# Heads of the second mixer normed among mLSTM tiles; w_ada tiles in the pauses of five norms

## Chip, cores, metric

One core of a Trainium2 chip. The metric is the device time of the whole program in microseconds, the median of several runs; lower is better. Everything is fp32 at the inputs and outputs.

## What is computed

A trunk of two layers over 256 tokens and 256 context tokens of width 1024, and then a second block. Cut to what matters:

```python
# first block, layer l = 0, 1
sh1, sc1, gt1, sh2, sc2, gt2 = split(silu(c) @ w_ada + b_ada, 6)      # for c and c_ctx
x = x + gt1 * (mix(modulate(rmsnorm(x, g1), sh1, sc1)) @ w_out)
x = x + gt2 * conv_ffn(modulate(rmsnorm(x, g2), sh2, sc2), w_up, conv_w, w_down)
...
x = rmsnorm(x, final_g)
# second block: its own w_ada; mLSTM in two directions and window attention, then PEER
h = modulate(rms(x, g), sh1, sc1);  p = h @ w_in
q, k = rope(rms(heads(p.q), q_g)), rope(rms(heads(p.k), k_g))
a = window_attention(q, k, v, kc, vc, sink);  m = mlstm(p)
x = x + g1 * ((sigmoid(g_m) * (m @ w_bm) + sigmoid(g_a) * (a @ w_ba)) @ w_out)
x = x + g2 * peer(modulate(rms(x, g'), sh2, sc2), w_query, keys, u, v)
```

## The kernel before, in words

Activations stand transposed, features on partitions, tokens along the free axis. Every large weight is read as tiles of 128 x 1024 fp32 (512 KB), one tile giving 128 output features over eight groups of 128 inputs. A product is made of three fp32r matmuls per group (`mm3`, L86): high times low, high times high, low times high parts. So each tile is *split* after it has landed: ScalarE rounds it into TH (`highs`), and VectorE or, for tiles flagged so, GpSimd subtracts into TL (`lows`). A tile takes 24 matmuls of 256 columns, or 48 with 512 tokens.

`weight_tiles` (L227) writes the order of all tiles by hand, and every engine's program follows it. SyncE issues all the transfers on one queue into RAW, a ring of four places (`sync_program`, L2518): tile i waits until tile i-4 has been split or, if it isn't split, used. TH and TL have three places each, and a split waits until the tile three splits before has been used by TensorE. `pool` in `add` says which tiles GpSimd subtracts.

The 144 tiles of w_ada (three blocks of 48) aren't split: each gives 8 plain fp32 matmuls with two stationary columns, all into one PSUM bank (`ada`). After each group of four, ScalarE copies the bank to AROW, and at the start of the next group TensorE and VectorE turn it into columns with the bias added (`columns`; a few groups, ADA_TURNED, L358, have that called elsewhere). `_ada_plan` (L333) says at which points of the program how many tiles stand: "head", "unit" (attention units), "between", "up" and "down" (feed-forward), "second", "heads", "lstm".

A norm: ScalarE squares eight rows, GpSimd adds the first five, TensorE sums over partitions with one-column matmuls (`norm`), VectorE adds epsilon (`above`), GpSimd takes the power -0.5 (`root`), TensorE spreads the root over partitions (`spread`), VectorE multiplies row by row (`norm_rows`), ScalarE modulates and rounds (`high_rows`), VectorE subtracts the low part. The next projections start with `project_side`, which takes three tiles' first rows together while the normed rows come.

The second mixer begins behind the final norm. `project_side` takes wg (gates), tile 20 (keys) and 21 (values); then come the query tiles 16 to 19. Each of the five heads' tiles (20, 16, 17, 18, 19; `HEAD_TILES`, L220) is copied by ScalarE, squared, summed (`head_stats`), gets its root on GpSimd, is spread (`head_spread`), normed by VectorE, and roped: a permuting matmul (`head_rope` on TensorE), then three VectorE operations. Before the change all of this stands in front of the attention units, in an order written out by hand in each engine's program (TensorE L922, ScalarE L1464, VectorE L2066, GpSimd L2499). The GpSimd program splits the next head's tile before it takes each root, if the tile is its.

Then come 16 attention units (`a_units`). In unit n TensorE turns the probabilities, does `scores2(n + 2)`, one mLSTM tile (`mlstm_tile(n)`, order `M_TILES`: four q, four output gates, four k, four v), one w_ada tile, and the product with the values. VectorE does `softmax2(n + 2)`, `keep2`, one step of the mLSTM recurrence (steps 0 to 4 in units 0 to 4), the copy of the tile, and `normal2(n + 2)`. Units 0 to 7 have tiles of 24 matmuls, 8 to 15 of 48. All PSUM banks but one are a ring of seven in program order. Each engine works strictly through its own program; semaphores connect them.

Line numbers in the rows are those of helpers: L79 and L84 are the matmuls, L107 transposes, L114 VectorE's or GpSimd's two-operand operation, L120 tensor_scalar, L126 scalar_tensor_tensor, L155 and L158 ScalarE's activation and copy, L2540 the weight transfers.

## Time and profile before

| | us |
|---|---|
| median of 3 runs | 2296.83 (2292.07, 2296.83, 2296.93) |
| the profiled execution's own time | 2286.08 |
| its span, first to last instruction | 2284.3 |
| TensorE busy | 2156.3 |
| VectorE busy | 1292.8 |
| ScalarE busy | 1088.5 |
| GpSimd busy | 488.4 |
| mean granted TensorE clock | 0.973 of full |

The span ends with 128 + 128 tiles of PEER experts, from about 1450 us on, in which TensorE is hardly ever idle. What the change touches lies between 287 and 1446 us. Busy times of TensorE are those of records whose ends are modelled, so consecutive matmuls overlap a little.

### The profile page before, as it was taken

How to read it: one execution, taken by the hardware profiler on the slowest of the kernel's cores; microseconds unless marked ns; L12 is line 12 of the kernel's file. 1: busy time of each engine (PE TensorE's matmuls, PEld its weight loads, DVE VectorE, ACT ScalarE, POOL GpSimd, SP SyncE). 2: the span in 40 equal slices, each digit the busy share in tenths (PEclk: the TensorE clock that was granted, in tenths of full speed). 3: DMA queues.
4: the chain of work that ended last, by engine and by line, in shares of the span. 5: the costliest groups of instructions: out<-in, count | busy, mean ns of one | idle time of the engine just before them, and what ended most of it. 6: DMA issues, size and time to landing. Idle time of an engine off the chain costs nothing.

```text
span 2284.3 us, 44523 instructions
## 1 busy us (share of the span) xinstructions
PE 2156.3 (94%) x19132; PEld 2030.5 (89%) x19132; DVE 1292.8 (57%) x2517; ACT 1088.5 (48%) x1880; POOL 488.4 (21%) x230
## 2 busy tenths in 40 slices
PE   4999999999999989998789998999999999999998
PEld 3977989999998779988668888999999999999998
DVE  2355454343344667555464455589568887666665
ACT  2343353232235446445333444565567776555554
POOL 0200100000002220001201343078866662000000
PEclk8999989999999999999879999999999999999999
DMA  7224323444454345764223334555544445555553
GB/s 279 76 101 155 123 93 130 163 152 166 167 171 151 125 154 181 247 231 137 77 93 130 129 102 150 165 185 188 182 139 148 148 140 174 187 186 189 187 185 130
DMA packets 97284, 355.01 MB, mean 155 GB/s; under 512 B 10688, under 2 KB 11712, under 8 KB 96704
## 3 DMA queue, kind: packets, MB, share of 16 engines
q1 hardware_dynamic: 97088, 352.18, 46.0%
q8 instruction: 150, 2.46, 0.4%
q14 instruction: 46, 0.38, 0.1%
HBM read 351.09 MB, written 1.05 MB: 154 GB/s over the span
## 4 chain that ended last, share of the span: by engine, by line
PE 82%; DVE 5%; issue 4%; ACT 4%; DMA 3%; POOL 2%; SPq 0%; ACTq 0%; DVEq 0%; POOLq 0%
PE ps L79 77%; PE ps L84 4%; ACT TH L158 2%; DVE TL L114 2%; POOL TL L114 1%; PE ps L107 1%; DMA RAW<-in_wdn 1%; DMA RAW<-in_wada 1%; ACT SQ L155 1%; DMA RAW<-in_wup 1%; POOL SM L114 1%; DMA RAW<-in_win 0%; ACT Hh L158 0%; DVE ps L114 0%; DVE X L126 0%
## 5 line engine op out<-in xcount | busy, mean ns | idle before, releaser
L158 ACT ACTIVATE TH<-RAW 128x1024 fp32r<-128x1024 f32 (+1 forms) x515 | 539.9, 1049 | 447.0 <-PE ps L79 190.8
L114 DVE TENSOR_TENSOR TL<-RAW,TH 128x1024 fp32r<-128x1024 f32 (+1 forms) x339 | 416.0, 1227 | 503.0 <-ACT TH L158 502.5
L114 POOL TENSOR_TENSOR TL<-RAW,TH 128x1024 fp32r<-128x1024 f32 x176 | 424.2, 2414 | 545.5 <-ACT TH L158 519.4
L79 PE MATMUL ps<-Hh,TL 128*128 128x256 f32 x1920 | 453.4, 289 | 42.3 <-ACT Hh L158 18.8
L79 PE MATMUL ps<-Hh,TH 128*128 128x256 f32 x1920 | 441.3, 282 | 0.0
L79 PE MATMUL ps<-Hl,TH 128*128 128x256 f32 x1920 | 440.5, 282 | 0.0
L79 PEld LDWEIGHTS ps<-Hh,TL 128*128 128x128 f32 x1920 | 325.0, 193 | 71.4 <-issue 30.5
L79 PE MATMUL ps<-HXh,TL 128*128 128x256 f32 x1312 | 365.6, 283 | 6.8 <-POOL TL L114 2.8
L79 PE MATMUL ps<-W,TH 128*128 128x256 f32 x2048 | 361.9, 281 | 0.0
L79 PE MATMUL ps<-HXh,TH 128*128 128x256 f32 x1312 | 360.0, 278 | 0.0
L79 PE MATMUL ps<-HXl,TH 128*128 128x256 f32 x1312 | 359.8, 278 | 0.0
L79 PEld LDWEIGHTS ps<-Hh,TH 128*128 128x128 f32 x1920 | 325.4, 193 | 0.7 <-issue 0.5
L79 PEld LDWEIGHTS ps<-Hl,TH 128*128 128x128 f32 x1920 | 325.2, 193 | 0.0
L79 PEld LDWEIGHTS ps<-W,TH 128*128 128x128 f32 x2048 | 312.5, 188 | 0.0
L79 PE MATMUL ps<-W,TL 128*128 128x256 f32 x1024 | 287.8, 281 | 1.5 <-DVE G L114 1.5
L79 PEld LDWEIGHTS ps<-HXh,TL 128*128 128x128 f32 x1312 | 246.8, 190 | 9.1 <-POOL TL L114 3.7
L79 PEld LDWEIGHTS ps<-HXh,TH 128*128 128x128 f32 x1312 | 246.0, 189 | 0.0
L79 PEld LDWEIGHTS ps<-HXl,TH 128*128 128x128 f32 x1312 | 245.5, 189 | 0.0
L79 PEld LDWEIGHTS ps<-W,TL 128*128 128x128 f32 x1024 | 196.6, 192 | 1.7 <-DVE G L114 1.7
L114 POOL TENSOR_TENSOR ACC<-SQ 128x512 f32<-128x512 f32 (+1 forms) x6 | 7.7, 1290 | 591.5 <-ACT SQ L155 591.5
L155 ACT ACTIVATE W<-W,T 128x128 fp32r<-128x128 f32 x256 | 82.0, 391 | 64.4 <-DVE W L114 64.4
L84 PE MATMUL ps<-RAW,SM 128*2 128x128 f32 x2304 | 93.7, 287 | 16.2 <-DMA RAW<-in_wada 16.2
(323 smaller groups left out, 3003.1 us busy)
## 6 DMA issues: line engine op xcount, KB each, us to landing
RAW<-in_wada SPq DMA_DIRECT2D x144, 512.0 KB, 3.6
RAW<-in_ut SPq DMA_DIRECT2D x128, 512.0 KB, 3.5
RAW<-in_v SPq DMA_DIRECT2D x128, 512.0 KB, 3.5
RAW<-in_wup SPq DMA_DIRECT2D x88, 512.0 KB, 4.4
RAW<-in_win SPq DMA_DIRECT2D x74, 512.0 KB, 4.4
RAW<-in_wdn SPq DMA_DIRECT2D x32, 512.0 KB, 4.4
RAW<-in_wout SPq DMA_DIRECT2D x24, 512.0 KB, 3.7
RAW<-in_wq SPq DMA_DIRECT2D x16, 512.0 KB, 4.3
```

What stands on the lines that cost most here:

```text
L79: return self.e.matmul(out, lhs, rhs, start=first, stop=last, skip_group_check=skip)
L84: return self.e.matmul(out, lhs, rhs, start=first, stop=last, tile_position=at)
L107: return self.e.transpose(out, src, eye)
L114: return DRY if self.e is None else self.e.tensor_tensor(out, a, b, op)
L155: return DRY if self.e is None else self.e.activation(out, a, fn, **kw)
L158: return DRY if self.e is None else self.e.activation(out, a, ACT.Copy, **kw)
```

## The change

It does two things. (1) Twelve w_ada tiles move into the pauses of five norms: two or one (`z` = 0) stand between a norm's sums and its spread, as many (`z` = 1) between the spread and the first projection. Layer 0's second norm has four, the other four norms (layer 1's first and second, the second block's first and second) two each. They come out of layer 0's up and down projections (4), layer 1's units (2) and down projections (4), the point "second" (1) and the mLSTM part (1). In these pauses ScalarE and VectorE split no tiles ahead for them. `columns(11)` is no longer called apart, and `columns(35)` stands behind the queries of PEER. (2) The heads of the second mixer: mLSTM tiles 0 and 1 come between the heads' tiles 17 and 18, head 3's norm begins before unit 0 and ends in unit 1, tile 19 with head 4 stands in units 0 to 3, and units 1 to 14 carry the other mLSTM tiles, unit 15 none. Of these tiles GpSimd splits 20 and every second one from tile 2 on; 16, 17, 0, 1, 18 and 19 are VectorE's, which also does the gate rows behind the first head's sum.

```diff
@@ weight_tiles
+    def gap(*norm):
+        for z in range(2):
+            ada("gap", *norm, z)
...
             add(("win", l, i), win[i], pool=2)
+            if l and i == 16:
+                gap("n1", l)
...
                 add(("wup", l, m), ins[f"wup{l}"][m])
+                if m == 1:
+                    gap("n2", l)
...
-    ada("second")
-    add(("wg",), ins["wg2"], pool=2)
-    for i in HEAD_TILES[0:1] + (21,) + HEAD_TILES[1:]:
-        add(("w2", i), w2[i], pool=2)
+    add(("wg",), ins["wg2"])
+    add(("w2", 20), w2[20], pool=1)
+    add(("w2", 21), w2[21])
+    gap("n1", 2)
+    for i in FILLS2[0:5]:
+        add(("w2", i), w2[i])
     ada("heads")
     for u in range(16):
-        add(("w2", M_TILES[u]), w2[M_TILES[u]], pool=2)
+        for i in fill2(u):
+            add(("w2", i), w2[i], pool=1 if u % 2 else False)
         ada("unit", 2, u)
...
+            if m == 2:
+                gap("n2", 2)
+FILLS2 = HEAD_TILES[1:3] + M_TILES[0:M_EARLY] + HEAD_TILES[3:5] + M_TILES[M_EARLY:]
+def fill2(u):
+    return FILLS2[5 + u:6 + u]
@@ tensor_program, at each of the five norms
+            ada("gap", "n2", l, 0)
             spread(("n2", l), ROOT[0][:, 0:NTB], 1, D, "h_norm", "m2", l, 7)
+            ada("gap", "n2", l, 1)
@@ tensor_program, second mixer
+        head_tile(1)
+        head_stats(0)
+        turn_rows(1, 4, (2, "vt", 0), A, "vt")
+        head_tile(2)
+        head_spread(0)
+        head_stats(1)
+        mlstm_tile(0)
+        head_rope(0)
+        head_spread(1)
+        head_stats(2)
+        mlstm_tile(1)
+        head_rope(1)
+        head_spread(2)
+        head_tile(3)
+        ada("heads")
+        scores2(0)
+        head_rope(2)
+        head_stats(3)
+        scores2(1)
         for n, (c, kv, qb) in enumerate(a_units):
...
-            mlstm_tile(n)
+            if n == 0:
+                head_tile(4)
+                head_spread(3)
+            elif n + M_EARLY <= 16:
+                mlstm_tile(n + M_EARLY - 1)
+            if n == 1:
+                head_rope(3)
+                head_stats(4)
+            elif n == 2:
+                head_spread(4)
+            elif n == 3:
+                head_rope(4)
@@ vector_program, second mixer
+        lows(at_tile["w2", 16])
+        head_above(0)
+        lows(at_tile["w2", 17])
+        for g in range(4):
+            gate_row(g)
+        lows(at_tile["w2", 0])
+        head_norm(0)
+        head_above(1)
+        head_rope(0)
+        lows(at_tile["w2", 1])
+        head_norm(1)
+        mlstm_tile(0)
+        head_above(2)
+        lows(at_tile["w2", 18])
+        head_rope(1)
+        head_norm(2)
+        mlstm_tile(1)
+        lows(at_tile["w2", 19])
+        ada("heads")
+        softmax2(0)
+        head_rope(2)
+        head_above(3)
+        softmax2(1)
+        normal2(0)
+        normal2(1)
         for n in range(16):
             if n + 2 < 16:
                 softmax2(n + 2)
             if n:
                 keep2(n - 1)
+            if n == 0:
+                head_norm(3)
+            elif n == 1:
+                head_rope(3)
+                head_above(4)
+            elif n == 2:
+                head_norm(4)
+            elif n == 3:
+                head_rope(4)
             if n < 5:
                 for d in range(2):
                     recurrence(d, n)
-            mlstm_tile(n)
+            for i in fill2(n):
+                lows(later(("w2", i), AHEAD))
+            if n and n + M_EARLY <= 16:
+                mlstm_tile(n + M_EARLY - 1)
@@ gpsimd_program
+        lows(at_tile["w2", 19])
         for c in range(5):
-            lows(at_tile["w2", HEAD_TILES[min(1 + c, 4)]])
             root(("head", c), ROOT[2 + c % 2][:, 0:4 if c else 8])
+            if c > 2:
+                lows(at_tile["w2", FILLS2[c + 3]])
```

ScalarE's program follows the same order.

## Rows read from the trace of the kernel before

**Rows 1.** The page's first part: busy us (share of the span), instructions.
```profile
PE 2156.3 (94%) x19132; PEld 2030.5 (89%) x19132; DVE 1292.8 (57%) x2517; ACT 1088.5 (48%) x1880; POOL 488.4 (21%) x230
```
**Rows 2.** TensorE's waits over the span: us in total, times, longest.
```profile
PE ps L79 <- POOL TL L114: 20.3, 8, 6.7
...
PE ps L107 <- DVE mprob L120: 5.7, 2, 4.0
```
**Rows 3.** Timeline at layer 1's first norm: start us, us, engine, instruction [idle before].
```profile
710.17 4.65 POOL L114 TENSOR_TENSOR TL<-RAW,TH 128x1024 fp32r<-128x1024 f32 x2
710.25 2.07 PE L79 MATMUL ps<-P,SM 128*128 128x128 f32 x8 [1.35 <-POOL SM L114]
...
712.54 2.64 SPq L2540 DMA_DIRECT2D RAW<-in_win  x3
...
715.08 0.77 PE L79 MATMUL ps<-Hh,TL 128*128 128x256 f32 x2 [2.75 <-ACT Hh L158]
```
**Rows 4.** Windows of lower clock at five norms: length, busy us per engine, clock, DMA.
```profile
709.53:719.77 10.24, 6.77 (x30) 6.50 (x31) 6.02 (x9) 6.56 (x13) 5.29 (x3) 0.50 0.44 155
...
1074.76:1081.59 6.83, 5.30 (x34) 4.44 (x35) 1.71 (x6) 1.79 (x4) 4.20 (x4) 0.50 0.00 1
...
sum 44.38, PE 31.90 PEld 30.18 DVE 25.89 ACT 27.25 POOL 11.42; mean PE 6.38 PEld 6.04 DVE 5.18 ACT 5.45 POOL 2.28
```
**Rows 5.** Windows: the heads' stretch; its last lower-clock stretch; all four of those.
```profile
1102.80:1193.50 90.70, 66.69 (x462) 51.09 (x460) 47.41 (x115) 28.52 (x56) 18.93 (x10) 0.77 0.23 76
...
1180.58:1190.81 10.23, 7.66 (x31) 5.74 (x32) 8.30 (x28) 4.22 (x12) 0.00 (x0) 0.50 0.16 51
sum 40.95, PE 29.39 PEld 22.37 DVE 17.02 ACT 10.00 POOL 6.13; mean PE 7.35 PEld 5.59 DVE 4.25 ACT 2.50 POOL 1.53
```
**Rows 6.** Timeline: one w_ada tile in dense work, one in a norm's pause.
```profile
680.03 0.62 PE L84 MATMUL ps<-RAW,SM 128*2 128x128 f32 x16
...
1080.16 1.03 PE L84 MATMUL ps<-RAW,SM 128*2 128x128 f32 x16
```
**Rows 7.** Transfers: issues of w_ada, KB each, median us to landing.
```profile
RAW<-in_wada SPq DMA_DIRECT2D x144, 512.0 KB, 3.6
```
**Rows 8.** Window in layer 1's down projections; the last number is GB/s.
```profile
984.00:1016.00 32.00, 28.78 (x324) 25.43 (x322) 11.89 (x17) 8.85 (x11) 0.00 (x0) 1.00 0.66 230
```
**Rows 9.** Timeline in front of head tile 17.
```profile
1098.49 3.22 DVE L126 SCALAR_TENSOR_TENSOR X<-X,SM,ps 128x256 f32<-128x256 f32 x8
...
1105.92 2.67 POOL L114 TENSOR_TENSOR SM<-SM 128x8 f32<-128x8 f32 x1 [22.51 <-DVE SM L120]
...
1110.95 0.58 PE L79 MATMUL ps<-Hh,TL 128*128 128x256 f32 x1 [6.71 <-POOL TL L114]
```
**Rows 10.** Timeline at head 0's rope: spread, rope operation, sums, a split by VectorE.
```profile
1120.95 0.66 PE L79 MATMUL ps<-P,SM 128*64 128x128 f32 x8
...
1121.13 0.42 DVE L114 TENSOR_TENSOR SQ<-ps,C 128x256 f32<-128x256 f32 x1 [3.06 <-PE ps L79]
...
1121.54 0.61 PE L79 MATMUL ps<-P,SQ 128*128 128x2 f32 x4
...
1122.73 1.21 DVE L114 TENSOR_TENSOR TL<-RAW,TH 128x1024 fp32r<-128x1024 f32 x1
```
**Rows 11.** The chain: start us, us, dense matmuls of 256 columns.
```profile
1912.75 362.06 PE ps L79 x3072
```
**Rows 12.** Timeline of the recurrence's second step in unit 2 and 3.
```profile
1168.91 0.41 DVE L120 TENSOR_SCALAR mkeep<-mkeep 4x512 f32<-4x512 f32 x1
...
1170.82 2.61 POOL L114 TENSOR_TENSOR TL<-RAW,TH 128x1024 fp32r<-128x1024 f32 x1 [29.95 <-ACT TH L158]
...
1171.31 2.66 DVE L114 TENSOR_TENSOR mvm<-mvm 4x512 f32<-4x512 f32 x1
...
1180.22 0.68 DVE L114 TENSOR_TENSOR mkm<-mkm 4x512 f32<-4x512 f32 x1
```

More of the change, by code:

```diff
@@ L220 @@
 HEAD_TILES = 20, 16, 17, 18, 19
+M_EARLY = 2
 class Box:
@@ L333, in _ada_plan, with gap @@
 def _ada_plan():
+    def gap(n, *norm):
+        return [(("gap",) + norm + (z,), n) for z in range(2)]
     plan = [(("head", 0), 8), (("head", 1), 8)]
     plan += [(("unit", 0, u), 24 * (u + 1) // 16 - 24 * u // 16) for u in range(16)]
+    plan += gap(2, "n2", 0)
     for third in range(3):
         for m in range(8 * third, min(8 * third + 8, 22)):
-            plan += [(("between", 0, m), 1)] * (m >= 12) + [(("up", 0, m), 1)]
-        plan += [(("down", 0, third, m), 1) for m in range(8)]
-    plan += [(("unit", 1, u), 10 * (u + 1) // 8 - 10 * u // 8) for u in range(8)]
-    plan += [(("down", 1, third, m), 1) for third in range(2) for m in range(8)]
-    plan += [(("second",), 1), (("heads",), 1)]
+            plan += [(("between", 0, m), 1)] * (m >= 12) + [(("up", 0, m), 1)] * (m > 1)
+        plan += [(("down", 0, third, m), 1) for m in range(8 if third < 2 else 6)]
+    plan += gap(1, "n1", 1)
+    plan += [(("unit", 1, u), 1) for u in range(8)]
+    plan += gap(1, "n2", 1)
+    plan += [(("down", 1, 0, m), 1) for m in range(8)] + [(("down", 1, 1, m), 1) for m in range(4)]
+    plan += gap(1, "n1", 2)
+    plan += [(("heads",), 1)]
     plan += [(("unit", 2, u), 1) for u in range(16)]
-    plan += [(("lstm", u), 1) for u in range(4)]
+    plan += [(("lstm", u), 1) for u in range(3)]
+    plan += gap(1, "n2", 2)
     at, n = {}, 0
@@ L1202, in ada, with gap @@
                     act.act(SC, par(["c1", "c2"][b]), ACT.Silu).then_inc(*A.mark("sc", b + 1))
+        def gap(*norm):
+            for z in range(2):
+                ada("gap", *norm, z)
         def stats(tag, src, t, *ready):
@@ L1517, in mlstm_tile @@
                 to_rows((2, "vm", c), ("w2", tile), 512, (c + 1) % 2, *free)
-        for n in range(2):
-            exps2(n)
+        head(0)
+        highs(at_tile["w2", 17])
+        to_rows((2, "vt", 0), ("w2", 21), 512, 1, (D, "h_low", "m1", 2, 7))
+        sq_read[1] = P, "row", 2, "vt", 0
+        highs(at_tile["w2", 0])
+        act.wait_ge(P, "row", 2, "vt", 0)
+        act.copy(m.vt, ps("row", 2, "vt", 0)[:, :].rearrange("p (b c) -> p b c", c=128)).then_inc(*A.mark("vt"))
+        head(1)
+        highs(at_tile["w2", 1])
+        head(2)
+        highs(at_tile["w2", 18])
+        highs(at_tile["w2", 19])
+        ada("heads")
+        head(3)
+        exps2(0)
+        highs(at_tile["w2", 2])
+        exps2(1)
         for n in range(16):
@@ L1695, in ada, with gap @@
                     columns(g)
+        def gap(*norm):
+            for z in range(2):
+                ada("gap", *norm, z)
         def scales(tag, l, name, part, slot):
@@ L2034, in vector_program, with gate_row @@
         dve.memset(m.ONE, 1.0).then_inc(*D.mark("one"))
-        for g in range(4):
+        def gate_row(g):
             d = g // 2
@@ L2170, in mlstm_tile @@
                 rows_v(c - 1)
-        for n in range(2):
-            softmax2(n)
-            normal2(n)
+        lows(at_tile["w2", 16])
[16 more added lines that the diff above has]
+        lows(at_tile["w2", 19])
+        ada("heads")
+        softmax2(0)
[4 more added lines that the diff above has]
+        normal2(1)
         for n in range(16):
```

101 lines of the change are left out of this document (27 added, 74 removed).

## The prediction, made before the change was run

> **What bounds the kernel now.** I read the page's first lines, then TensorE's waits over the span, then the norms' timelines and granted clock, last the stretch with the second mixer's heads. TensorE is busy 2156.3 us, the next engine, VectorE, 1292.8 [rows 1]. So the time is TensorE's own work, what it waits for, and what its work loses while the lower of the clock's two levels (1.2 instead of 2.4 GHz) is granted. Its largest wait is for splits made by GpSimd, 20.3 us in eight waits; the one for normalised probabilities is 5.7 in two, of which one is 4.0 and so the other 1.7 [rows 2]. Two places hold most of what can be won.
>
> The norms: TensorE idles before the root comes and again before the first normed row, 1.35 and 2.75 us at layer 1's first norm [rows 3]. Around the five norms that the change touches the clock is at its lower level for 44.4 us, in which TensorE is busy 31.9 [rows 4]. Dense work loses half of its time there, one-column sums less; I put the loss at 12 us.
>
> The heads: from 1102.8 to 1193.5 TensorE is busy 66.7 of 90.7 us, so it idles 24.0. In four stretches at the lower clock it is busy 29.4, of which half, 14.7, is loss [rows 5]. Together 38.7 us.
>
> The profiled execution took 2286.1 us, 1.8 more than its span and 10.7 below the median of the three runs, 2296.8. The sum is made against 2286.1, and the gain is then taken off the median. About 0.2% (4.6 us) is what a measurement of this kernel can tell from no change.
>
> **Part 1: w_ada tiles in the pauses.** Twelve of the 144 tiles stand in pauses afterwards. One (called second) did already, so eleven leave dense stretches. A tile is 0.62 us long there [rows 6], less the 0.07 by which records of TensorE overlap (a spread from 1120.95 takes 0.66 and the next matmul is there at 1121.54 [rows 10]): 11 x 0.55 = 6.0 us. In a pause it costs nothing as long as the wait beside it is longer. At the lower clock it takes 1.03 [rows 6], and the pauses before and after the spread are 1.35 and 2.75 [rows 3]; layer 0's has two tiles in each half, which the cover just holds. The cover is GpSimd's root and the first rows of VectorE and ScalarE; if it went, the eleven tiles would cost what they cost now.
>
> A tile must also have landed. RAW has four places, so the second tile of a pause takes the place of the norm's first weight tile once that is split. In front of the up projections, of the second mixer and of wq VectorE makes that split before the root is asked for, and a w_ada tile lands 3.6 us after its issue [rows 7]: in time. At layer 1's first norm GpSimd makes it, behind the root: two splits back to back in 4.65 us from 710.17, the first done at 712.5, where SyncE issues the next tile [rows 3]. The pause's second tile then lands at 716.1 and takes 1.0: the projections begin at 717.2 instead of 715.08. **Cost 2.1 us**; bounds 0 (it lands sooner) and 3 (the low clock goes on for as long again over dense work). What is behind it on SyncE's queue is weights not needed for 30 us.
>
> Layer 1's down projections carry 12 tiles instead of 16. They move 230 GB/s and idle 3.2 of 32 us [rows 8]. I give the relief of the transfers 1 us, between 0 and 2.
>
> The clock in the pauses: at the one norm that has a tile in its pause the lower level ended at 1081.59, with the pause's own work; at layer 1's first norm, with none, it went on to 719.77, over 4.7 us of dense work from 715.08 [rows 3, 4, 6]. So a filled pause gives the clock back earlier. The ends are 0 and 12 us. I take 4, because the one-column sums ahead of the root, in which it falls, stay.
>
> **Part 2: the heads among the tiles.** TensorE's work stays; what changes is what each split waits for.
> - Tile 17. VectorE did eight rows of the final norm (3.22 us) and the gate rows before the first head's sum; GpSimd took the root (2.67) and then the split, and TensorE waited 6.71 for it until 1110.95 [rows 9]. Now VectorE makes the split directly behind that sum, and the gate rows follow. The sum's matmuls end about 1103.7, sum and split take 1.4, TensorE arrives at 1104.2: wait 1.1. Queued behind are tile 0's split (in time with TensorE, bank 0.3 late) and the recurrence, not needed yet.
> - Tile 18 before, tile 1 now. VectorE has a rope (3 x 0.42) and the split (1.21) to do behind TensorE's rope matmul, while TensorE has a spread and sums, 0.66+0.61 [rows 10]: wait 1.2. Behind that rope waits tile 1's split and so one RAW place; TensorE then has tile 1 to do, 24 matmuls at 362.06/3072 us, 2.8 [rows 11].
> - Unit 0. A rope (1.3) stands between VectorE's two first softmaxes now: 1.7 becomes 3.0 [rows 2, 10].
> - Unit 4. The recurrence's second step holds VectorE from 1168.91 to 1180.90, and TensorE waited 4.0 for the probabilities behind it [rows 2, 12]. Now VectorE must first norm head 4, whose spread comes behind a tile (2.8+0.66 after the scores; it started 1.6 after them), and do tile 13's split: about 2.4 and 1.2 more, against a spread and a rope more on TensorE, 1.2. **Wait 6.4.** But one addition of the step took 2.66 where its twin took 0.68, beside a split of 2.61 on GpSimd [rows 12]. Tile 12's split comes earlier now, so I expect that back: 4.4. Between them I take 5.5.
> - The recurrence's columns, needed by TensorE right after unit 4's scores: 1.0.
>
> Waits 1.1+0.3+1.2+3.0+5.5+1.0 = 12.1 instead of 24.0: 11.9 saved. Clock: unit 4's fall stays (half of 7.66 busy, 3.8 [rows 5]); of falls at tile 17 and at unit 0 I count one, 3.4: 7.2 instead of 14.7, 7.5 saved. The part brings 19.4. Ends: 9 (waits nearly as before, or the clock) and 27.
>
> On that addition of 2.66: the Trainium skill (SBUF — State Buffer, section "SBUF: two separate sides") says that VectorE, with two SBUF inputs, and GpSimd take their shared port pair as a lock for a whole instruction. The trace agrees: the addition ended 0.5 us after the split did. By the rule the wait is 4.4 and the sum 1 us better; with the delay put down to chance it is 6.4 and 1 us worse.
>
> **Sum.** 6.0 - 2.1 + 1 + 4 + 19.4 = 28.3 us: 2257.8 for an execution like the profiled one, **2269** against the median.
>
> **Rivals.**
> A, *VectorE paces the heads.* Its queue alternates ropes, which wait for TensorE, with splits, for which TensorE waits. With 3 us at each of five heads, 3 at unit 0, 8.5 at unit 4 and 1 behind it, waits are 27.5, and with 11 of clock the heads bring nothing. Part 1 is left, 9 us: 2288. For it: VectorE works 47.4 of the 90.7 us [rows 5] and gets three more splits. Against: its split takes half of GpSimd's. Chance 0.13.
> B, *slower: the clock stays down through the head units.* Place: tile 17 to unit 4. TensorE's work at full speed is 52 us (90.7 - 38.7). If attention's part-array matmuls and short waits keep the lower level throughout, that is 104, plus 12 of waits: 26 more than now, less 9 from part 1: 2314. It decides from some 70 us of lower clock on; now there are 41 [rows 5]. Against: three tiles in a row are dense work. Chance 0.06.
> C, *the clock holds*: only unit 4's fall is left in the heads, and the pauses get most of theirs back: 28 + 3 + 8 = 39, and 2 from shorter waits: 2256. Chance 0.13.
> D, *every pause tile is late* by a landing, 3.6: 18 less at five norms, 2287. Against: where VectorE splits, the place is free in time. Chance 0.06.
>
> **How the numbers follow.** The forecast has 0.62; its own range is 2259 to 2282, for its terms' bounds don't all fall on one side. To leave out no more than 2 in 10 the range takes in C, D and A: 2255 to 2288. Faster by over 0.2% (below 2292.2) are the forecast, C, D and A, less something for a mishap I can't see: 0.87. Same 0.06. Slower, B and a remainder, 0.07.
>
> **What would show it.** Right: the two long waits for GpSimd's splits (6.71 and its neighbour) gone; the heads' stretch, measured to the same tile, 19 us shorter; a wait of 4 to 7 us for normalised probabilities at unit 4; a wait of 1 to 2 us for RAW<-in_wada at layer 1's first norm and at no other; low-clock stretches at the norms shorter than 44.4 in sum. Wrong: waits of 2 us and more for VectorE's splits at tiles 0, 1 and 18; the lower level over most of the units; waits for w_ada at several norms.

## The result, and the profile after

| | before | after |
|---|---|---|
| median, us | 2294.45 (4 runs, 2289.30 to 2296.93) | 2260.76 (4 runs, 2259.18 to 2263.05) |
| profiled execution, us | 2286.08 | 2259.43 |
| its span, us | 2284.3 | 2257.6 |

After / before is 0.9859, 95% interval 0.9839 to 0.9879: 33.7 us by the medians, 26.65 by the two profiled executions (that of before lay 8.4 under its median). So 7 us of the gain by the medians stand in no trace: what follows explains the 26.65. The forecast was 2269 in 2255 to 2288, and a gain of 28.3 in the profiled execution.

The page's first part of the changed kernel, to be laid beside [rows 1]:

```profile
PE 2152.4 (95%) x19132; PEld 2028.1 (90%) x19132; DVE 1298.6 (58%) x2521; ACT 1088.5 (48%) x1880; POOL 479.4 (21%) x226
```

TensorE's busy time fell by only 3.9 us. The rest is idle time, and TensorE's waits over the span of the changed kernel (us in total, times, longest) say where it was:

```profile
PE ps L84 <- DMA RAW<-in_wada: 19.1, 10, 10.9
PE ps L79 <- DVE TL L114: 15.4, 19, 1.5
...
PE ps L79 <- POOL TL L114: 6.8, 5, 3.8
...
PE ps L79 <- ACT AROW L158: 5.4, 5, 3.8
PE ps L79 <- DVE mst L114: 4.9, 1, 4.9
PE ps L107 <- DVE mprob L120: 4.8, 1, 4.8
...
PE ps L79 <- DVE ADA L114: 1.2, 1, 1.2
```

Two of these lines in the kernel before:

```profile
PE ps L79 <- DVE TL L114: 14.0, 18, 1.3
...
PE ps L79 <- ACT AROW L158: 8.3, 8, 3.7
```

The waits for GpSimd's splits went from 20.3 to 6.8 us [rows 2]. VectorE's splits, which took them over, cost hardly more than before: 15.4 us instead of 14.0. The waits for ScalarE's copy of a w_ada row (AROW) fell from 8.3 to 5.4. The last line is a wait that the forecast did not have.

**Where the time went.** The best ruler is the start of the same work in both traces. Each line below is the distance between two such marks in us (first matmul of a norm's sums, first matmul of the product behind it, and so on).

| stretch | before | after | difference |
|---|---|---|---|
| layer 0's second norm's product to layer 1's first norm | 410.45 | 403.95 | -6.50 |
| four norms' pauses ahead of the second mixer (sums to first product) | 40.34 | 41.05 | +0.71 |
| layer 1's attention units | 135.76 | 132.05 | -3.71 |
| layer 1's down projections | 162.17 | 159.73 | -2.44 |
| the rest ahead of the second mixer | | | +0.24 |
| **second mixer's first product to first mLSTM scores (heads)** | 199.49 | 182.55 | **-16.94** |
| scores to the query tiles | 156.03 | 155.12 | -0.91 |
| query tiles to keys | 46.98 | 48.14 | +1.16 |
| keys to the last layer's first tile | 7.14 | 8.58 | +1.44 |
| from there to the end | | | +0.28 |

So the first part of the change brought 11.7 us up to the second mixer, the heads brought 16.9, and 2.0 were lost behind them.

The heads' stretch as a window (length, then busy us of PE, PEld, DVE, ACT, POOL, clock, DMA share, GB/s), of the kernel before and of the changed one:

```profile
1083.66:1283.15 199.49, 175.48 (x1431) 145.78 (x1431) 95.03 (x230) 74.79 (x143) 34.60 (x17) 0.90 0.30 105
```
```profile
1071.96:1254.51 182.55, 169.66 (x1431) 142.70 (x1432) 99.85 (x233) 76.03 (x144) 28.93 (x14) 0.94 0.34 116
```

PE is TensorE, PEld its weight loads, DVE VectorE, ACT ScalarE, POOL GpSimd. Length less PE's busy time is what PE idled: 24.0 before, 12.9 after. The same 1431 matmuls are busy 5.8 us less, with the mean clock at 0.94 instead of 0.90.

What ends the two long waits that are left there? The timeline at unit 0 (start, us, engine, instruction, idle before):

```profile
1120.04 2.34 POOL L114 TENSOR_TENSOR TL<-RAW,TH 128x1024 fp32r<-128x1024 f32 x1
1120.14 0.15 DVE L120 TENSOR_SCALAR mst<-mst 128x1 f32<-128x1 f32 x1
1120.22 2.18 DVE L114 TENSOR_TENSOR mst<-mst 128x1 f32<-128x1 f32 x1
...
1122.63 0.49 DVE L120 TENSOR_SCALAR mprob<-mprob,mst 128x512 f32<-128x512 f32 x1
...
1123.17 1.11 PE L107 MATMUL ps<-P,mprob 128*128 128x128 f32 x4 [4.81 <-DVE mprob L120]
```

An addition of one column, 0.15 us elsewhere, took 2.18 and ended with GpSimd's split of mLSTM tile 2 (1122.40 and 1122.38). And at unit 3's end, on VectorE, then on TensorE:

```profile
1150.89 0.41 DVE L120 TENSOR_SCALAR mkeep<-mkeep 4x512 f32<-4x512 f32 x1
1151.33 0.68 DVE L114 TENSOR_TENSOR mkeep<-mkeep,mkm 4x512 f32<-4x512 f32 x1
...
1155.86 1.21 DVE L114 TENSOR_TENSOR TL<-RAW,TH 128x1024 fp32r<-128x1024 f32 x1
1157.00 0.40 DVE L129 COPY mqm<-ps 128x256 f32<-128x256 f32 x1
1157.33 0.14 DVE L114 TENSOR_TENSOR mst<-mst 128x1 f32<-128x1 f32 x1
```
```profile
1152.07 0.62 PE L84 MATMUL ps<-RAW,SM 128*2 128x128 f32 x16
1157.55 0.66 PE L79 MATMUL ps<-mpp,mvt 128*64 128x128 f32 x2 [4.86 <-DVE mst L114]
```

The profile puts this wait down to the one-column operation at 1157.33. The value product does not read that; it needs a bank. Banks go round in a ring of seven, and the one that it takes was last taken for mLSTM tile 3, seven places earlier in TensorE's program. The copy mqm<-ps, which frees that bank, stands just ahead of the one-column operation, behind the recurrence's second step for both directions and a split.

Layer 1's first norm in the changed kernel:

```profile
703.11 4.66 POOL L114 TENSOR_TENSOR TL<-RAW,TH 128x1024 fp32r<-128x1024 f32 x2
...
705.47 0.33 SPq L2614 DMA_DIRECT2D RAW<-in_wada  x1
...
709.06 0.61 PE L84 MATMUL ps<-RAW,SM 128*2 128x128 f32 x8 [3.98 <-DMA RAW<-in_wada]
```

The second pause tile is issued when GpSimd's first split ends and is there 3.6 us later; the pause, sums to first product, is 11.81 instead of 9.99.

### The profile page after: what moved, and what is told of

It is laid out like the page before. It is cut to its first block, busy times and chain, and to the rows that moved or that the text cites. A ratio compares the mean times of both kernels' runs of the same rounds, so it can differ in the third digit from the quotient of the medians.

```text
span 2257.6 us, 44527 instructions
## 1 busy us (share of the span) xinstructions
PE 2152.4 (95%) x19132; PEld 2028.1 (90%) x19132; DVE 1298.6 (58%) x2521; ACT 1088.5 (48%) x1880; POOL 479.4 (21%) x226
## 3 DMA queue, kind: packets, MB, share of 16 engines
HBM read 351.09 MB, written 1.05 MB: 156 GB/s over the span
## 4 chain that ended last, share of the span: by engine, by line
PE 85%; DVE 5%; ACT 3%; DMA 3%; issue 2%; POOL 2%; SPq 0%; ACTq 0%; DVEq 0%; POOLq 0%
PE ps L79 79%; PE ps L84 4%; DVE TL L114 2%; ACT TH L158 2%; PE ps L107 1%; DMA RAW<-in_wada 1%; POOL TL L114 1%; DMA RAW<-in_wdn 1%; ACT SQ L155 1%; DMA RAW<-in_wup 1%; POOL SM L114 0%; ACT Hh L158 0%; DVE ps L114 0%; DMA RAW<-in_win 0%; DVE SQ L114 0%
## 5 line engine op out<-in xcount | busy, mean ns | idle before, releaser
L114 DVE TENSOR_TENSOR TL<-RAW,TH 128x1024 fp32r<-128x1024 f32 (+1 forms) x343 | 421.0, 1228 | 477.8 <-ACT TH L158 477.3
L114 POOL TENSOR_TENSOR TL<-RAW,TH 128x1024 fp32r<-128x1024 f32 x172 | 414.0, 2410 | 522.3 <-ACT TH L158 496.0
```

What stands on the lines that cost most here:

```text
L114: return DRY if self.e is None else self.e.tensor_tensor(out, a, b, op)
```

## The experiments

The kernels of the experiments ran in three batches, each on one chip beside runs of the kernel before. Those runs spread from 2273.9 to 2299.2 us, so causes are read from distances in the traces, and the ratios only say whether the end agrees. "Heads" below is the stretch of the table, 199.49 before and 182.55 after. The distances of each kernel in us; the last column is how long the lower clock was granted within the heads:

| kernel | ratio to before (95%) | heads | PE idle | PE busy | lower clock |
|---|---|---|---|---|---|
| before | 1 | 199.49 | 24.0 | 175.5 | 41.0 |
| after | 0.9859 (0.9839 to 0.9879) | 182.55 | 12.9 | 169.7 | 20.6 |
| heads_only | 0.9909 (0.9877 to 0.9941) | 182.57 | 13.9 | 168.7 | 17.1 |
| gaps_only | 0.9938 (0.9910 to 0.9965) | 202.40 | 23.9 | 178.5 | 48.6 |
| n11_one | 0.9865 (0.9829 to 0.9901) | 182.31 | 12.9 | 169.4 | 20.4 |
| tile2_swap | 0.9889 (0.9863 to 0.9915) | 183.37 | 11.9 | 171.5 | 23.9 |
| cols35_early | 0.9849 (0.9798 to 0.9900) | 181.75 | 13.0 | 168.7 | 17.1 |
| rec_spread | 0.9843 (0.9792 to 0.9894) | 180.20 | 11.6 | 168.6 | 17.1 |
| dense | 0.9813 (0.9762 to 0.9864) | 185.01 | 12.7 | 172.3 | 27.3 |
| comb | 0.9816 (0.9777 to 0.9856) | 180.10 | 12.2 | 167.9 | 13.7 |
| rec_late | 0.9854 (0.9832 to 0.9876) | 178.87 | 9.1 | 169.8 | 20.7 |
| no_pool | 0.9861 (0.9840 to 0.9882) | 184.43 | 12.3 | 172.1 | 27.2 |
| all | 0.9828 (0.9804 to 0.9852) | 177.06 | 8.9 | 168.2 | 13.7 |
| all_dense | 0.9827 (0.9812 to 0.9841) | 176.93 | 8.6 | 168.3 | 13.7 |

Five of these kernels have the same order of work in the heads: after, heads_only, n11_one, cols35_early and dense. Four have heads between 181.75 and 182.57; in dense, whose profiled execution lay 25 us above its median, they are 185.01, with 27.3 us of lower clock. Ahead of unit 0, where rec_spread and rec_late have that order too, the distance from the first product is 48.6 to 51.2 us, at nearly the same waits, so by the clock. A difference of 1 to 3 us in the heads is therefore not by itself an edit's doing. What tells more is PE's idle time (12.7 to 13.9 in those five) and the distance from unit 0's first matmul to unit 6's, called units 0 to 5 below (50.4 to 50.5 in three of the five, 51.4 in heads_only, 53.9 in dense).

### The two parts alone

heads_only is the changed kernel with the w_ada plan of the kernel before and its places for the two steps that turn rows into columns:

```diff
-    plan += gap(2, "n2", 0)
...
-    plan += gap(1, "n1", 2)
-    plan += [(("heads",), 1)]
+    plan += [(("second",), 1), (("heads",), 1)]
...
-ADA_TURNED = (3, 9, 35)
+ADA_TURNED = (3, 9, 11, 35)
```

> The kernel before with only the second mixer's heads moved (and the split ring's shares there); every w_ada tile stands where it stood before. Theory A, the two parts add up as the traces divide them: the heads part is worth 16.9 us in the two traces (11.7 us of lead at the second mixer's first projection, 28.6 us at its first mLSTM scores), so this kernel is 15 to 19 us faster than the kernel before (some 2275 to 2279 against 2294), with the same four waits among the head tiles as the changed kernel (tile 1 about 1.4, unit 0 about 4.8, unit 4 about 4.9 us) and three stretches of low clock from 1100 us on, not six. Theory B, the heads part lives on the first part's relief (w_ada tiles gone from the queue, another phase of the clock): under 12 us of gain. The tile of w_ada columns stays where it stood, so the 1.2 us wait at the keys for a bank is absent.

Heads 182.57, 16.92 shorter than before, against 16.94 in the changed kernel; ahead of the second mixer it stands 1.3 us behind the kernel before. By the ratio 21 us (14 to 28). Its waits at tile 1, unit 0 and unit 3's end are the changed kernel's (1.39, 4.80 and 4.95), and it has no wait at the keys. Theory A.

gaps_only is the kernel before with those lines the other way round and the `gap` calls; the second mixer's order and the shares of its splits stay:

```diff
-    plan += [(("second",), 1), (("heads",), 1)]
+    plan += gap(1, "n1", 2)
+    plan += [(("heads",), 1)]
...
+            ada("gap", "n2", l, 0)
             spread(("n2", l), ROOT[0][:, 0:NTB], 1, D, "h_norm", "m2", l, 7)
+            ada("gap", "n2", l, 1)
```

> The kernel before with only the w_ada tiles moved into the pauses of the five norms. Theory A, additive: the two traces give this part 11.7 us up to the second mixer's first projection, so 10 to 14 us faster than the kernel before, of which 6.0 are eleven tiles at 0.55 us, the rest the clock in the pauses and a wait of 1.06 us before the columns that is gone; the late second tile at layer 1's first norm costs 2 us as in the changed kernel. Theory B, the runs' medians (33.7 us apart, where the two profiled executions are 26.7 apart) hide more here than the trace shows: 15 us or more. Theory C, below 6 us: what the tiles save in the pauses comes back in the second mixer, whose order is as before.

Up to the second mixer's first product 9.3 us shorter (1013.27 against 1022.52; 1011.55 in the changed kernel), then the heads are 2.9 longer than before, at an idle time of 23.9 as before: that is clock, 48.6 us of the lower level instead of 41.0. It ends 3.5 us ahead in the profiled execution, 14 (8 to 21) by the ratio. The distance up to the mixer is just short of theory A's, the ratio within it, the profiled end nearer C. At the last norm ahead of the mixer the pause is 14.86 us, against 12.19 in the changed kernel. GpSimd's timeline there and then TensorE's:

```profile
1066.48 4.66 POOL L114 TENSOR_TENSOR TL<-RAW,TH 128x1024 fp32r<-128x1024 f32 x2
```
```profile
1065.89 2.08 PE L79 MATMUL ps<-P,SM 128*128 128x128 f32 x8
1072.45 1.03 PE L84 MATMUL ps<-RAW,SM 128*2 128x128 f32 x16 [4.48 <-DMA RAW<-in_wada]
```

With the old shares GpSimd makes two of this norm's three splits, behind the root (one of 2.35 us in the changed kernel), and the second pause tile comes late as at layer 1's first norm. So the new shares of the mixer's splits serve the first part as well; otherwise the parts add: 16.9 + 9.3 = 26.2 in distances, and 0.9909 x 0.9938 = 0.9848 against 0.9859 in ratios.

### Layer 1's first norm

```diff
-    plan += gap(1, "n1", 1)
-    plan += [(("unit", 1, u), 1) for u in range(8)]
+    plan += gap(1, "n1", 1)[0:1]
+    plan += [(("unit", 1, u), 9 * (u + 1) // 8 - 9 * u // 8) for u in range(8)]
```

> The changed kernel, but at layer 1's first norm only one w_ada tile stands in the pause; the other goes back into that layer's attention units (9 tiles on 8 units). Theory A, the second tile's load came late (PE waited 3.98 us for it, where the rows alone would have let it start some 2.1 us earlier): the pause gets 2.1 us shorter, the tile costs 0.6 to 0.7 us dense in a unit, so 1 to 2 us faster than the changed kernel. Rival B, the load that was late was late for the ring, not for its place: the next tile's split now waits in its stead and the pause stays 11.8 us long, the tile's 0.6 us is added: 0.5 to 1 us slower.

The pause is 9.82 us, 2.0 shorter than in the changed kernel and 0.2 shorter than before; the units behind it are 1.05 longer (133.10 against 132.05): they hold the tile's 0.6, and the lower clock reaches 5.2 us past their start instead of 3.6. The wait for the tile is gone, which is theory A's mechanism; the gain is 0.9 us in distances, just under its 1 to 2 and too little for the ratio to show.

### VectorE beside GpSimd

```diff
-            add(("w2", i), w2[i], pool=1 if u % 2 else False)
+            add(("w2", i), w2[i], pool=1 if u == 2 or u > 1 and u % 2 else False)
```

> The changed kernel, but the split of mLSTM tile 2 is VectorE's and that of tile 3 GpSimd's. Theory A, VectorE's one-column operation of the second softmax took 2.17 us beside GpSimd's split of tile 2 because the two engines hold each other up, and it ends unit 0's wait of 4.8 us: without GpSimd there it takes 0.2 us and unit 0's wait falls to 2.7 to 3.3 us, 1.5 to 2 us faster than the changed kernel in that unit, part of it given back where VectorE has 1.3 us more work before the next softmax. Rival B, the operation waited for something else (its input or ScalarE): it is 2 us long again, wherever tile 2 is split. Rival C, tile 3's split now meets another chain in unit 1 or 2 and the 2 us come back there: end within 0.5 us of the changed kernel.

VectorE's timeline at the same place, with no split on GpSimd beside it:

```profile
1121.21 0.15 DVE L120 TENSOR_SCALAR mst<-mst 128x1 f32<-128x1 f32 x1
1121.28 0.15 DVE L114 TENSOR_TENSOR mst<-mst 128x1 f32<-128x1 f32 x1
...
1121.66 0.49 DVE L120 TENSOR_SCALAR mprob<-mprob,mst 128x512 f32<-128x512 f32 x1
```

The addition takes 0.15 again and unit 0's wait 2.77 instead of 4.81: theory A for the mechanism. But the heads come out at 183.37, 0.8 longer. PE idles 1.0 less and is busy 1.8 more: GpSimd's split of tile 3 now makes it wait 1.1, and the lower clock behind unit 3's wait lasts 13.65 us, not 3.41, while that at unit 0 lasts 6.83, not 10.24. The end looks like rival C, by the clock more than by another wait. But the 13.65 are not shown to come of the edit: dense, with the changed kernel's own order there, has them too behind the same wait, though in its long execution.

no_pool takes the splits of units 1, 3 and 5 from GpSimd altogether (`pool=1 if u > 6 and u % 2`):

> The changed kernel, but VectorE splits the mLSTM tiles of units 1, 3 and 5 too, so GpSimd splits none in the first six units. A split costs VectorE 1.2 us; what it costs VectorE when GpSimd does it (2.3 us) depends on what stands beside it. Theory A, the two engines hold each other up in additions and one-column operations (0.15 us became 2.17 and 1.30, an addition of 0.68 became 2.75 in the run with swapped splits): unit 0's wait falls from 4.8 to some 2.8 us, and VectorE's three added splits cost less than the hold-ups, so unit 6 starts 99 to 100.5 us after the second mixer's first projection against 101.6. Rival B, VectorE is short there, and 3.7 us more work in six units shows in full: 101.5 to 104.

Unit 0's wait is 2.77 again, the heads 184.43: in rival B's range (unit 6 at 103.5), but not shown to be by its cause. Of that cause there is a new wait of 1.65 in unit 2, for VectorE's copy of a tile. Still PE idles 0.6 less than in the changed kernel; it is busy 2.5 more. Behind unit 3's wait, which is unchanged at 4.86, stands this window of lower clock:

```profile
1153.76:1167.41 13.65, 11.06 (x46) 8.90 (x46) 11.75 (x33) 5.17 (x12) 0.00 (x0) 0.50 0.16 53
```

It is as long as in dense and in tile2_swap. So whether it pays to take the splits from GpSimd stays open.

### The recurrence

rec_spread moves the second direction's second step from unit 2 to 3 (and its later steps by one):

```diff
...
-            if n < 5:
-                for d in range(2):
-                    recurrence(d, n)
+            for d in range(2):
+                if n < 5 + d and (not d or n != 2):
+                    recurrence(d, n - 1 if d and n > 2 else n)
```

> The changed kernel, but the second direction's scan step of the recurrence runs one unit later, so VectorE has one direction's six operations (4.2 us) in unit 2 and one in unit 3, not both in unit 2; what follows of that direction moves one unit too. Theory A, VectorE's load in units 2 and 3 (both recurrences with a head's norm and the rotary steps) makes PE wait 4.9 us in unit 4: that wait falls under 1.5 us, the low clock behind it (3.4 us) goes, and the first mLSTM scores come 4 to 6 us earlier against the second mixer's first projection (182.6 us in the changed kernel). Rival B, VectorE is short over the whole of units 0 to 5, and the wait only moves to units 3 to 5 in smaller pieces: under 2 us of gain. Rival C, the wait is for the bank that VectorE's copy of an mLSTM tile frees; the copy sits behind the recurrence in either place: 2 to 4 us.

The 4.86 us wait is gone. Against the second mixer's first product unit 4 starts 8.4 us earlier than in the changed kernel, but unit 6 only 2.2. PE waits 0.6, 0.7, 1.3 and 1.0 in units 4 and 5 instead, and a second stretch of 3.4 us of lower clock comes. The heads are 180.20, 2.35 shorter, but 2.6 of it were there at unit 0's probabilities already, ahead of the edit (the lower clock of the norm, and a stretch of 3.41 us behind tile 1's wait, are absent there). Units 0 to 5 take 50.7 us, against 50.4. That is rival B: within units 0 to 5 the wait only moves.

rec_late leaves one direction in unit 2 and puts the other into units 8 to 10:

```diff
...
-            if n < 5:
-                for d in range(2):
-                    recurrence(d, n)
+            for d in range(2):
+                if n < 2 or n in (8 - 6 * d, 9 - 6 * d, 10 - 6 * d):
+                    recurrence(d, n if n < 2 or d else n - 6)
```

> The changed kernel, but only the second direction's scan step stays in unit 2; the first direction's runs in unit 8, its later steps in units 9 and 10, where units last 9 us and VectorE works some 5 of them. Theory A, in units 0 to 5 VectorE is short as a whole (spreading the two steps over units 2 and 3 only moved the 4.9 us wait of unit 4 to units 4 and 5): 4.2 us of scans less in the first six units make PE's 4.9 us go and stay gone, and unit 6 starts 98 us after the second mixer's first projection or earlier, against 101.6 in the changed kernel, and the first mLSTM scores 178 or earlier against 182.6. Rival B, the late step holds up units 8 to 10 by as much as it frees in unit 4: scores at 181 to 183. Rival C, the units' length is set by PE and the clock, not by VectorE: the 4.9 us go but 2 to 3 us of low clock remain wherever they fall, scores at 179 to 181.

Units 0 to 5 as a window, of the changed kernel and of rec_late:

```profile
1123.17:1173.53 50.36, 45.30 (x360) 34.73 (x361) 36.46 (x88) 22.56 (x46) 5.90 (x3) 0.90 0.31 105
```
```profile
1125.65:1172.02 46.37, 45.02 (x356) 34.82 (x356) 31.54 (x78) 22.96 (x46) 6.94 (x4) 0.89 0.33 114
```

VectorE's busy time falls by 4.9 us, the stretch by 4.0, PE's busy time by 0.3. Unit 6 starts 97.6 us after the first product (theory A wanted 98 or less), and units 6 to 15 take 81.3 instead of 81.0, so the late step costs next to nothing. The heads are 178.87, 3.7 shorter, with PE idle for 9.1 us, well below the 12.7 to 13.9 of the kernels with the changed kernel's order. So it is work of VectorE that held these units up, as theory A says, and taking it out brings PE's idle time back. Theory A's second figure, 178 at the scores, is missed by 0.9: a stretch of 3.41 us of lower clock stays in unit 4, as rival C has it, and 178.87 lies at the edge of C's 179 to 181. Part of the 4.0 may also be GpSimd's: in the changed kernel a one-column addition in unit 4 takes 2.33 us beside a split, here none does. The ratio, 0.9854, does not set the kernel apart from the changed one.

### The last columns

```diff
             project_side([("wq", c) for c in range(3)], ..., together=5)
+        columns(35)
         for c in range(3, 16):
             project(("wq", c), hx, 256, h3, A, "pq", c)
-        columns(35)
```

> The changed kernel, but the step that turns the last w_ada row into columns stands behind the third query tile on PE and behind the kept copy on VectorE, ahead of the splits for the keys. Theory A, the changed kernel loses 2.6 us between its second norm's first product (29.55 us ahead of the kernel before) and the first tile of the last layer (26.93 us ahead) because VectorE reaches that addition late and a bank is held: PE's wait of 1.18 us ahead of the keys and the low clock behind it go, and the stretch from the query tiles to that first tile comes 1.2 to 2.6 us shorter. Rival B, the loss is in the two pause tiles' loads or the clock's phase: the stretch (56.7 us in the changed kernel, 54.1 before) stays within 0.5 us.

Keys to the last layer's first tile take 7.14 us as before (8.58 in the changed kernel): theory A for those 1.4. The rest did not come. Query tiles to keys stay at 48.2, now with a wait of 1.39 for a split that stands behind the early columns on VectorE. heads_only, with the order of before there, took 46.43, but n11_one, with the changed kernel's, took 46.42: the 1.16 us of the table are scatter as far as these runs show.

### Filling the pauses

```diff
+        def keep_busy(o, n):
+            for _ in range(n):
+                pe.mm(o[:, :], ones, PT[:, 0:512], True, True, True)
```
One call with n = 1 ahead of the wait for the root, one with n = 2 behind the spread, at each of the five norms.

> The changed kernel with matmuls that compute nothing used in the pause of each of the five norms: one of 512 columns ahead of the wait for the root, two behind the spread of it (the results are written over). Theory A, the granted clock falls for 6.8 to 10.2 us at each of the five norms because PE's matmuls there are one column wide or PE waits; matmuls of 512 columns in the gaps keep it up or bring it back one stretch (3.4 us) sooner: 41 us of low clock in the five pauses fall to under 25, for 2 to 8 us of gain. Rival B, the clock falls on what PE did in the one-column sums before the root, so the matmuls behind it come too late: the stretches stay as they are and the added matmuls, at the low clock some 1.7 us for each 512 columns, delay the rows: 3 to 10 us slower.

The profiled execution (2272.1 us) was 25 above this kernel's median (2246.8), and longer than the changed kernel's in stretches that the edit does not touch (163.9 against 159.7 in layer 1's down projections), so only the pauses are read. The lower clock of the pauses falls from 41.0 us to 17.1: at layer 0's second norm and at the second mixer's 6.8 us are there, at layer 1's first 3.4 of 10.2, at the other two none. The pauses themselves, sums to first product, became 1.7, 0.5 and 1.3 us longer at three norms, 0.4 shorter at one, and stayed at the last. The clock goes as theory A says; whether it pays, this run doesn't tell, and the pair at the end is to.

### Together

comb: n11_one, cols35_early, tile2_swap and rec_spread in one.

> The changed kernel with four edits: one w_ada tile at layer 1's first norm, the last columns early, tile 2's split on VectorE and tile 3's on GpSimd, the recurrence's scan step spread over two units. If the sources of loss are separate, their gains add: 1 at the norm, 1.2 to 2.6 at the keys, 4 to 6 in unit 4, and the 2.0 us of unit 0's wait, which the third run gave back in unit 4, are kept: 8 to 11 us ahead of the changed kernel where the last layer's first tile starts (1466.4 us there, so 1455 to 1459). If VectorE is short over units 0 to 5 as a whole, the last two give under 3 us together: 1461 to 1464.

The last layer's first tile starts at 1462.5, 3.9 ahead of the changed kernel: not in the range of the added gains, but in the second, 1461 to 1464. The two edits in units 0 to 5 gave 2.5 in the heads, no more than one alone, and even this is mostly clock (13.7 us of the lower level instead of 20.6; PE idles only 0.7 less). The failed sum is what sent the recurrence to unit 8. The split that moved to tile 3 now met an addition of the recurrence:

```profile
1153.40 2.44 POOL L114 TENSOR_TENSOR TL<-RAW,TH 128x1024 fp32r<-128x1024 f32 x1 [12.57 <-ACT TH L158]
...
1153.62 2.76 DVE L114 TENSOR_TENSOR mkeep<-mkeep,mkm 4x512 f32<-4x512 f32 x1
```

> The changed kernel with four edits: one w_ada tile in the pause of layer 1's first norm (1 us), the last columns behind the sixth query tile on PE and three splits later on VectorE than in the run that had them early (2.6 us; that run got 1.4 and showed a new wait of 1.4 us for a split behind the early columns), the first direction's scan step in unit 8, and no splits by GpSimd in units 1 to 5. If the causes are as read so far, the last layer's first tile starts some 9 to 12 us earlier than in the changed kernel (1466.4 there): 1454 to 1458. If VectorE or the clock takes back the units' part: 1460 to 1463.

1464.4, which misses both ranges. The heads are, with those of all_dense, the shortest: 177.06, 5.5 shorter than in the changed kernel, by 4.0 us less idle time and 6.9 less of the lower clock. rec_late has the same idle time to 0.2 us, so the splits taken from GpSimd show no gain of their own here. The keys give their 1.4 and layer 1's norm 2.0; but layer 1's attention units took 136.60, where n11_one and comb, with the same order there, took 133.10 and 132.98 (PE idles 1.4 more than in comb, and 3.3 us more are at the lower clock). With that scatter out, it would be 1460.9.

> The kernel of the run named all, with the three filling matmuls in each norm's pause. Theory A, they shorten the low clock in the five pauses (from 41 us to some 20 in the run that had them alone) and pay: the same distances between marks (norm to norm) come 1 to 3 us shorter per pause than in the run all, 3 to 8 us in sum at the last layer's first tile. Rival B, what they win in clock they take in time (1.7 to 2.5 us a pause ahead of the rows): within 2 us of the run all, either way.

From layer 0's first product to the last layer's first tile it takes 1402.35 us, against 1403.62 in the run all. But 3.0 us are lost ahead of the first filled pause, where nothing was edited; from there on (layer 0's second norm's sums) it is 1176.96 against 1181.27, so 4.3 shorter. The window of layer 1's first norm shows the mechanism, first all, then all_dense:

```profile
697.00:712.00 15.00, 11.46 (x87) 10.87 (x87) 7.84 (x14) 8.11 (x15) 5.65 (x3) 0.70 0.38 138
```
```profile
697.00:712.00 15.00, 13.41 (x113) 11.40 (x112) 7.51 (x13) 7.98 (x14) 5.65 (x3) 1.00 0.27 95
```

The lower clock of 10.2 us is gone there, and the 6.8 at layer 1's second norm and at the last one too; at layer 0's second norm 3.4 are left of 6.8. At the second mixer's norm the pause got 2.4 longer and the lower level lasted 10.2 us instead of 6.8. In sum the lower clock of the five pauses went from 37.6 us to 13.7. What that brings is a matter of which distances are counted. Each pause together with the stretch behind it changed by +0.2, -3.4 (all's long attention units), +1.5, +2.3 and -1.3 us: 0.7 us shorter in sum, rival B's range. Of the other 3.6 us, 3.2 lie in layer 1's down projections (161.91 and 158.72 us), a stretch without an edit that takes 157.21 to 163.94 in the kernels with the same tiles there. With them it would be theory A's 3 to 8. By the ratios, 0.9828 and 0.9827, there is no gain. So filling matmuls do hold the clock up in four pauses of five, and a gain from it is not shown.

## Why the prediction was right, point by point

The forecast was 8 us above the median, and in the profiled execution 28.3 against 26.65 measured. The two mechanisms are the right ones: filled pauses, and splits that no longer wait for GpSimd. That the sum is within 1.7 us is in part luck. Up to the second mixer came 2.8 us more than the 8.9 of part 1, in the heads 2.5 less than their 19.4, and behind them 2.0 were lost that the forecast did not have. Three views of the changed kernel's lower clock, which the points below use: the stretch at the norm ahead of the second mixer, the sum of the stretches at the five norms (as in [rows 4]), and the sum of those that begin among the heads (as in [rows 5]):

```profile
1065.23:1075.47 10.24, 8.54 (x60) 6.94 (x53) 6.35 (x12) 5.32 (x10) 4.75 (x3) 0.50 0.41 154
...
sum 40.96, PE 32.76 PEld 26.80 DVE 26.93 ACT 25.35 POOL 11.13; mean PE 6.55 PEld 5.36 DVE 5.39 ACT 5.07 POOL 2.23
```
```profile
sum 17.08, PE 13.59 PEld 11.13 DVE 10.18 ACT 5.12 POOL 4.45; mean PE 4.53 PEld 3.71 DVE 3.39 ACT 1.71 POOL 1.48
```

- **Eleven tiles, 6.0 us; relief, 1.** Up to the second mixer 11.7 us came. Layer 0's second half gave 6.5: four tiles are 2.2 of it; the lower clock, which had gone on 5.3 us behind the first product (to 299.94), ended at 293.82, ahead of it, for half of 5.3; and 1.06 were a wait for ScalarE's row at the columns that the change moved. Layer 1's units gave 3.7: two tiles are 1.1, such a wait at columns 1.04, and they have 4.5 us less of lower clock, of which 3.41 are one stretch that the run all has again. The down projections gave 2.4: four tiles are 2.2, and PE idles 1.4 less, of which 0.92 are a wait at columns and so 0.5 at most the relief of the transfers; a new stretch of 3.41 us of lower clock took about 1.7 back. The three waits at columns, 3.0 us, are a gain that the prediction never priced. They go with the places of the w_ada tiles: heads_only has them (1.67, 1.04, 0.79), gaps_only does not.
- **The clock in the pauses, 4.** About half of it came. The lower level lasts 41.0 us at the five norms instead of 44.4, and TensorE is busy 32.8 us in it instead of 31.9. What costs is the part behind the first product, over dense work: 20.2 us before, 16.1 after, so some 2 us are won. That a filled pause ends the lower level earlier holds at layer 0's second norm. At the second mixer it is the other way round: the level ended 2.1 us ahead of the product before (1081.59, product at 1083.66), and reaches 3.5 us past it now (1075.47, product at 1071.96).
- **The late tile, 2.1.** The pause grew by 1.82, with the issue where it was predicted, just behind GpSimd's first split, and it was the only norm of the five with a wait for w_ada. n11_one confirms the cause, gaps_only that it is GpSimd's split behind the root that makes a tile late.
- **The waits among the heads, 12.1.** Measured, with the forecast in brackets: tile 17 0.90 (1.1; the prediction's own times, 1103.7 + 1.4 against 1104.2, make 0.9), bank 0.60 (0.3), tile 1 1.39 (1.2), unit 0 4.81 (3.0), unit 4 4.86 (5.5), columns none (1.0): 12.6 in sum. Here too the errors cancel. The term that failed in size is unit 0: the rope is there as priced, and beside it stood a hold-up of 2.0 us by GpSimd's split, shown by tile2_swap and no_pool. The Trainium skill's rule (SBUF — State Buffer, section "SBUF: two separate sides") was weighed at unit 4 alone, where no split met the addition (0.68 us), as forecast; it should have been laid against every two-input VectorE operation beside a moved split. Unit 4's wait came just ahead of that unit and was for a bank, not for probabilities, with the same VectorE work in front.
- **The clock among the heads, 7.5.** PE's busy time fell by 5.8. At the lower level it is busy 13.6 us in the stretches that begin among the heads, of which half, 6.8, is loss against 7.2 forecast. But the norm's stretch now reaches 3.5 us into the heads, for another 1.75: 8.5 in all, and from 14.7 that is a fall of 6.2, close to the 5.8. So the rule that half of the busy time is lost holds well, and what the forecast lacked is the norm's stretch. Its 7.2 is also made otherwise than measured: behind unit 4's wait 1.6 (3.8 forecast), at tile 1 and unit 0 5.2 (3.4 forecast, for one of the two).
- **Not foreseen:** the columns moved behind the keys' splits, which cost 1.4 us. cols35_early gives them back, and heads_only, with the columns at their old place, does not lose them. The prediction asked at tile 17, tile 1 and on SyncE's queue what stands behind a moved step, but not for these columns: which splits stand ahead of them on VectorE, and who waits for the bank.
- **Rivals.** A (VectorE paces the heads) holds in units 0 to 5 alone, for the 4 us that rec_late took away. B did not come: there are 20.6 us of lower clock in the heads, where it needed 70. C wanted only unit 4's fall left there; beside it (3.41) are one of 3.41 and one of 10.24 us. D's late tiles came at one norm of five.

## What to carry to other kernels

Ask of each moved step who waits for its output on the other engine, and what stands on the two engines that can hold each other up during every split that moves with it. Where one engine is short over several units, take work out of those units altogether; spreading it within them only moves the wait. Judge changes of some microseconds by distances between the same marks in two traces, look how much such a distance scatters among kernels that are the same there, and do not add gains that sit on one queue. When a stretch gets shorter or longer, take its idle time and its time at the lower clock apart before naming a cause.

## What the runs showed of the hardware

**The last product runs at one of two speeds in kernels whose code is the same there**, at a granted clock of 1.00 in both. Its windows in the changed kernel and in n11_one (matmuls in brackets):

```profile
2050.00:2100.00 50.00, 50.00 (x427) 50.00 (x426) 30.54 (x36) 28.99 (x36) 0.00 (x0) 1.00 0.59 185
```
```profile
2050.00:2100.00 50.00, 50.00 (x444) 50.00 (x443) 32.29 (x38) 28.98 (x37) 0.00 (x0) 1.00 0.62 196
```

427 matmuls in 50 us are 117 ns each, 444 are 113. The 3072 matmuls take 362.05 us or 348.42, 13.6 apart, and nothing in between: 348.42 in n11_one, cols35_early, rec_spread, rec_late and all, 362.05 in the rest, before and after among them. No edit touches it. It is a large part of the differences between the ends of the profiled executions. Each kernel has one trace, so whether one kernel shows both speeds is not shown, and what sets the speed stays open.

**A one-column addition on VectorE can take 2.3 us.** It takes 0.15 alone and 2.18 beside a split on GpSimd, as an addition of 4 x 512 takes 0.68 or 2.76. The changed kernel has a second case, in unit 4:

```profile
1162.13 2.39 POOL L114 TENSOR_TENSOR TL<-RAW,TH 128x1024 fp32r<-128x1024 f32 x1 [17.70 <-ACT TH L158]
1162.21 2.33 DVE L114 TENSOR_TENSOR mst<-mst 128x1 f32<-128x1 f32 x1
```

In every such case from 1050 to 1300 us, in all traces, the one-column addition ends 0.01 to 0.02 us after the split and the addition of 4 x 512 0.54 to 0.55 after it; one that starts late in a split takes 0.38 to 0.72. So the hold-up goes by what is left of the split, not by the operation's own size. Operations with one of their two inputs in PSUM are not held up: in the changed kernel one of 128 x 256 (ps<-mtmp,ps, at 1282.95) takes 0.43, its usual time, within a split that runs from 1281.41 for 2.37.

**The same wait costs more or less clock.** Unit 3's wait of 4.9 us was followed by 3.41 us at the lower level in the changed kernel, heads_only, n11_one and cols35_early, and by 13.65 in tile2_swap and no_pool, and also in dense, which has the changed kernel's order there (its execution was the long one). The waits are the same to 0.1 us. So an edit that saved 1.0 us of waiting, tile2_swap, came out with 1.8 us more of busy time. What the edits did to this, and what is scatter, stays open.
